# Grouped-query attention on one Trainium2 core: where the softmax's inverse sums are applied, and in which order TensorE does a unit's work

## What is computed

```python
def block_gqa_attention(q, k, v):
    ...
    def one_block(qb):
        s = jnp.einsum('bqkgd,bskd->bkgqs', qb, k).astype(jnp.float32) * scale
        p = jax.nn.softmax(s, axis=-1).astype(v.dtype)
        return jnp.einsum('bkgqs,bskd->bqkgd', p, v)
```

## Time and profile before

| what | value |
|---|---|
| median of 3 runs | 3661.1 us (3657.92 to 3663.45) |
| span of the profiled execution | 3665.8 us |
| this stage, first score product to last output | 1451.9 to 1843.2 us |
| TensorE, whole program | busy 3414.6 us, 93% of the span |
| VectorE, whole program | busy 1622.0 us, 44% |
| ScalarE, whole program | busy 815.3 us, 22% |
| GpSimd, whole program | busy 366.0 us, 10% |
| LDWEIGHTS (PEld), whole program | busy 1749.2 us, 48% |

### The profile page before, as it was taken

One profiled execution on the slowest core, in us unless ns is written; L12 is line 12 of the kernel. 1 busy time (PEld: TensorE's weight loads), 2 busy tenths in 40 slices (PEclk: granted clock), 3 DMA queues, 4 the chain that ended last, 5 costly groups with the idle time before them and its releaser, 6 DMA issues. The chain is left out here.

```text
span 3665.8 us, 51705 instructions
## 1 busy us (share of the span) xinstructions
PE 3414.6 (93%) x20940; PEld 1749.2 (48%) x20940; DVE 1622.0 (44%) x2578; ACT 815.3 (22%) x1819; POOL 366.0 (10%) x355
## 2 busy tenths in 40 slices
PE   9999999898999799999998999998899979898996
PEld 4444665533333344777755333333455658554332
DVE  4750886511111475777756110113342875563214
ACT  0000660100000122555510000000333551110112
POOL 0010300210000000000000200000000820003110
PEclk9999999899999999999998999999999989999998
DMA  9990211699999621000024999997322302229996
GB/s 370 359 346 1 93 70 69 274 389 427 426 424 425 239 89 62 22 1 1 1 92 184 380 426 427 426 424 308 130 82 79 139 17 87 95 98 347 420 417 264
DMA packets 146709, 818.45 MB, mean 223 GB/s; under 512 B 29763, under 2 KB 35651, under 8 KB 100390
## 3 DMA queue, kind: packets, MB, share of 16 engines
q1 hardware_dynamic: 117910, 737.25, 50.3%
q0 software_dynamic: 25824, 68.88, 4.9%
q10 hardware_dynamic: 2736, 8.95, 0.6%
HBM read 752.56 MB, written 82.56 MB: 228 GB/s over the span
## 5 line engine op out<-in xcount | busy, mean ns | idle before, releaser
L2415 PE MATMUL m_yp<-m_w,m_hidT 128*32 128x512 f32 (+2 forms) x2248 | 378.5, 595 | 10.3 <-issue 4.3
L2392 PE MATMUL m_up<-m_w,m_xT 128*32 128x512 f32 (+2 forms) x1792 | 313.9, 612 | 36.3 <-DMA m_w<-in_moe_w_up 33.9
L2392 PE MATMUL m_gp<-m_w,m_xT 128*32 128x512 f32 (+2 forms) x1792 | 297.4, 594 | 4.7 <-DVE m_xT L1978 2.9
L2143 DVE TENSOR_TENSOR m_hid<-m_sg,m_up 128x512 f32<-128x512 f32 x42 | 28.9, 688 | 561.4 <-PE m_up L2392 561.4
L2138 DVE TENSOR_TENSOR m_yt<-m_yp,keep_flat 128x512 f32<-128x512 f32 x128 | 82.5, 687 | 392.5 <-PE m_yp L2415 391.7
L2415 PEld LDWEIGHTS m_yp<-m_w,m_hidT 128*32 128x32 f32 (+2 forms) x2248 | 121.7, 124 | 219.0 <-issue 213.5
L2392 PEld LDWEIGHTS m_up<-m_w,m_xT 128*32 128x32 f32 (+2 forms) x1792 | 106.7, 127 | 238.4 <-issue 238.3
L2476 ACT ACTIVATE m_sg<-m_gp 128x512 f32<-128x512 f32 (+1 forms) x64 | 33.5, 524 | 759.7 <-PE m_gp L2392 515.2
L434 PE MATMUL front_acc<-front_hT,front_wt 128*128 128x512 f32 x448 | 194.7, 594 | 0.4 <-DVE q0T L535 0.4
L1233 PE MATMUL n_acc<-n_wt,n_hT 128*128 128x512 f32 (+2 forms) x512 | 191.2, 529 | 2.1 <-DMA n_wt<-in_w_in 1.4
L2392 PEld LDWEIGHTS m_gp<-m_w,m_xT 128*32 128x32 f32 (+2 forms) x1792 | 97.7, 123 | 198.2 <-issue 194.6
(11 more groups left out here) (520 smaller groups left out, 5037.4 us busy)
## 6 DMA issues: line engine op xcount, KB each, us to landing
m_w<-in_moe_w_gate SPq DMA_DIRECT2D x64, 2048.0 KB
m_w<-in_moe_w_up SPq DMA_DIRECT2D x64, 2048.0 KB
m_w<-in_moe_w_down SPq DMA_DIRECT2D x64, 2048.0 KB
v<-in_ada_w SPq DMA_DIRECT2D x40, 1024.0 KB
m_w<-in_moe_w_gate SPq DMA_DIRECT2D x32, 1024.0 KB
m_w<-in_moe_w_up SPq DMA_DIRECT2D x32, 1024.0 KB
m_w<-in_moe_w_down SPq DMA_DIRECT2D x32, 1024.0 KB
v<-in_w_mod SPq DMA_DIRECT2D x24, 1024.0 KB
```

What stands on the lines that cost most here:

```text
L2392: last = pe.matmul(acc[part, 0:F], xT[:, j, k, part], w[:, place_of[m_, r][0], k * F:(k + 1) * F], start=k == 0, stop=k == KC - 1)
L2415: last = pe.matmul(yp[e][part, :], hidT[:, k, part], w[:, place_of["d", r][0], k * D + e * 512:k * D + (e + 1) * 512], start=k == 0, stop= ...
```

## The change

The inverse sums are applied earlier and by another engine, and the order within a unit is another one:

- GpSimd, idle in this stage before, multiplies each head's row of 1024 exponentials in place by its inverse sum, two instructions a unit. TensorE's fills wait for that (`n_ready`) and no longer for the exponentials.
- VectorE's reciprocal is one column for each head, one instruction a head (before: one of 128 columns for a unit).
- The transpose of the inverse sums, ScalarE's copy of them (`spread`) and the buffer `inv_rows` are gone. VectorE's last step is a plain copy (`copy_out`) in place of the multiplication.
- TensorE's order is `score(n+1)`, all four fills of unit n, `combine(n-1)`. Fill 3 goes into the bank of fill 0, behind its copy. ScalarE copies fills 0 and 3, VectorE fills 1 and 2; ScalarE's copy of fill 0 of unit n now stands ahead of the exponentials of unit n+1.
- The maximum of the first head is taken in two halves and joined by a reduction of two columns: the first half starts when half of that head's scores are there (`s_half`).

```diff
                 def turn_probs(n):
+                    if n:
+                        copied(pe, n - 1, range(4))
+                    for f, bank in enumerate(BANKS):
+                        if f % 2 == 0:
+                            pe.wait_ge(n_ready, 2 * n + f // 2 + 1)
+                        if f == 3:
+                            copied(pe, n, (0,))
...
                 score(0)
                 for n in range(UNITS):
                     if n + 1 < UNITS:
                         score(n + 1)
-                    for i in range(3):
-                        turn_probs(n, i)
+                    turn_probs(n)
                     if n:
                         combine(n - 1)
-                    turn_probs(n, 3)
                 combine(UNITS - 1)
...
-                    pe.wait_ge(r_ready, n + 1)
-                    pe.transpose(out[:, P:2 * P], inv[:, n % 2].rearrange("p h w -> p (h w)"), ident[:, :]).then_inc(pv_done, 1)
...
+                    dve.wait_ge(s_half, n + 1)
+                    dve.tensor_reduce(parts[:, n % 2, 0:1], scores[0][:, 0:HALF], AX.X, ALU.max).then_inc(part_max, 1)
+                    dve.wait_ge(s_ready, 2 * n + 1)
+                    dve.tensor_reduce(parts[:, n % 2, 1:2], scores[0][:, HALF:], AX.X, ALU.max).then_inc(part_max, 1)
+                    dve.wait_ge(part_max, 2 * n + 2)
+                    dve.tensor_reduce(top[:, n % 2, 0:1], parts[:, n % 2], AX.X, ALU.max, negate=True).then_inc(max_ready, 1)
+                    dve.wait_ge(s_ready, 2 * n + 2)
+                    dve.tensor_reduce(top[:, n % 2, 1:2], scores[1][:, :], AX.X, ALU.max, negate=True).then_inc(max_ready, 1)
+
+                def inverse(n, h):
+                    dve.wait_ge(p_ready, 2 * n + h + 1)
+                    dve.reciprocal(inv[:, n % 2, h:h + 1], total[:, n % 2, h:h + 1]).then_inc(inv_ready, 1)
...
                     if n + 1 < UNITS:
                         row_max(n + 1)
-                    evacuate_probs(dve, n, 0, dve.tensor_copy)
-                    evacuate_probs(dve, n, 2, dve.tensor_copy)
+                    evacuate(dve, n, 1, dve.tensor_copy, evac_v)
+                    if n + 1 < UNITS:
+                        inverse(n + 1, 0)
+                    evacuate(dve, n, 2, dve.tensor_copy, evac_v)
+                    if n + 1 < UNITS:
+                        inverse(n + 1, 1)
                     if n:
-                        scaled_out(n - 1)
-                    if n + 1 < UNITS:
-                        inverse(n + 1)
-                scaled_out(UNITS - 1)
+                        copy_out(n - 1)
+                copy_out(UNITS - 1)
...
                 exponentials(0)
                 for n in range(UNITS):
+                    evacuate(act, n, 0, copy, evac_s)
                     if n + 1 < UNITS:
                         exponentials(n + 1)
-                    evacuate_probs(act, n, 1, copy)
-                    if n:
-                        spread(n - 1)
-                    evacuate_probs(act, n, 3, copy)
-                spread(UNITS - 1)
+                    evacuate(act, n, 3, copy, evac_s)
+
+            @block.gpsimd
+            def _(pool):
+                for n in range(UNITS):
+                    for h in range(2):
+                        pool.wait_ge(inv_ready, 2 * n + h + 1)
+                        pool.tensor_scalar(probs[:, n % 2, h], probs[:, n % 2, h], inv[:, n % 2, h:h + 1], None, ALU.mult).then_inc(n_ready, 1)
```

More of the change, by code:

```diff
@@ L128, in pair_attention, with copied @@
         probs = st.sb("probs", [P, 2, 2, S])
-        probsT = st.sb("probsT", [P, 2, 2, TILES, P])
+        probsT = st.sb("probsT", [P, 2, 2 * TILES * P])
+        parts = st.sb("parts", [P, 2, 2])
         top = st.sb("top", [P, 2, 2])
         total = st.sb("total", [P, 2, 2])
-        inv = st.sb("inv", [P, 2, 2, HEAD])
-        inv_rows = st.sb("inv_rows", [P, P])
+        inv = st.sb("inv", [P, 2, 2])
         scores = [st.ps(f"scores{h}", [P, S]) for h in range(2)]
-        turn = [st.ps(f"turn{b}", [P, 512]) for b in range(TURN)]
+        turn = [st.ps(f"turn{b}", [P, 512]) for b in range(3)]
         out = st.ps("out", [P, 512])
         ahead_in = st.sem("ahead_in")
[L138 to L148, removed]
+        s_half, s_ready, part_max, max_ready, p_ready = (st.sem(n) for n in ("s_half", "s_ready", "part_max", "max_ready", "p_ready"))
+        inv_ready, n_ready = st.sem("inv_ready"), st.sem("n_ready")
+        t_done, evac_v, evac_s = st.sem("t_done"), st.sem("evac_v"), st.sem("evac_s")
+        pv_done, o_done = st.sem("pv_done"), st.sem("o_done")
+        BANKS, BY_ACT, BY_DVE = (0, 1, 2, 0), (0, 3), (1, 2)
+        def copied(eng, n, fills):
+            for done, mine in ((evac_s, BY_ACT), (evac_v, BY_DVE)):
+                count = sum(f in fills for f in mine)
+                if count:
+                    eng.wait_ge(done, len(mine) * n + max(i for i, f in enumerate(mine) if f in fills) + 1)
         with st.block() as block:
@@ L159, in _ @@
             def _(pe):
[L160 to L165, removed]
                 def score(n):
@@ L173, in score, with turn_probs @@
                                 pe.wait_ge(p_ready, 2 * (n - 1) + h + 1)
-                            last = pe.matmul(scores[h][:, c * 512:(c + 1) * 512], qT[half, j, t * P:(t + 1) * P],
-                                             kT[half, 2 * j // SHARE, c * 512:(c + 1) * 512], start=True, stop=True)
+                            last = pe.matmul(scores[h][:, c * HALF:(c + 1) * HALF], qT[half, j, t * P:(t + 1) * P],
+                                             kT[half, 2 * j // SHARE, c * HALF:(c + 1) * HALF], start=True, stop=True)
                             if c == 1:
                                 last.then_inc(s_ready, 1)
[L179 to L183, removed]
+                            elif h == 0:
+                                last.then_inc(s_half, 1)
+                def turn_probs(n):
+                    if n:
[5 more added lines that the diff above has]
+                            copied(pe, n, (0,))
+                        for m in range(4):
+                            k = f % 2 * 4 + m
+                            last = pe.transpose(turn[bank][:, m * P:(m + 1) * P], probs[:, n % 2, f // 2, k * P:(k + 1) * P], ident[:, :])
+                        last.then_inc(t_done, 1)
                 def combine(n):
@@ L219, in row_max, with copy_out @@
                 def row_max(n):
[L220 to L229, removed]
+                    dve.wait_ge(s_half, n + 1)
[9 more added lines that the diff above has]
+                    dve.reciprocal(inv[:, n % 2, h:h + 1], total[:, n % 2, h:h + 1]).then_inc(inv_ready, 1)
+                def copy_out(n):
                     j, t = n // TILES, n % TILES
-                    dve.wait_ge(rb_done, n + 1)
-                    dve.tensor_tensor(natural[:, j, t], grid(out[:, 0:P]), grid(inv_rows[:, :]), ALU.mult).then_inc(o_done, 1)
+                    dve.wait_ge(pv_done, n + 1)
+                    dve.tensor_copy(natural[:, j, t], out[:, 0:P].rearrange("p (r c) -> p r c", c=GRID_W // TILES)).then_inc(o_done, 1)
                 row_max(0)
-                inverse(0)
+                for h in range(2):
+                    inverse(0, h)
                 for n in range(UNITS):
```

27 lines of the change are left out of this document (10 added, 17 removed).

## The result

The changed kernel takes 3722.97 us (median of four runs), beside 3662.27 us for the kernel before: the ratio is 1.0154, 95% interval 1.014 to 1.0168. One of the four runs was a slow one (4232.4 us, at a mean granted clock of 0.789 where the others have 0.962); it counts in the median and not in the ratio. By the medians the change costs 61 us, by the ratio 56 (51 to 62), where 12.5 us less was forecast; 3722.97 lies above the range, which ended at 3690.

A forecast was written before the change was run, and what follows sets the result against it. TensorE was taken to bound the kernel at 5.97 us a unit; 63 x 0.19 = 12.0 and 0.5 at the stage's end gave -12.5 us, so 3648.6 us, range 3644 to 3690.

The forecast's parts named there:

- What bounds the kernel, and TensorE's unit: TensorE bounds the stage at 5.97 us a unit; turning and split fills go, saving 0.19 (0.17 to 0.21), leaving 5.78.
- The clock of one unit: Times after a unit's scores start: first exponential 3.11, first reciprocal to 4.9, GpSimd 5.0, next scores 5.78 us.
- G: GpSimd's time for one multiplication of 128x1024, two a unit; taken as 1.3 us.
- 4.03 + G: Unit time in us once the third fill waits for GpSimd's second multiplication; as long as before, 5.97, at G = 1.94.
- The border of 1.73: Value of G in us under which GpSimd's second multiplication is hidden; beyond it the third fill waits.
- G, bounded: GpSimd's multiplication estimated from other rows: 1.16 from below, 2.5 from above, 1.3 us taken, nearer to MEMSET.
- The prediction's other estimate, 1.84 us: GpSimd's multiplication at about 1.8 cycles an element at 1.2 GHz, with 0.3 us fixed; unit 5.87, sum near -6 us.
- The sum: Whole kernel: 63 x 0.19 = 12.0 and 0.5 at the stage's end, -12.5 us, giving 3648.6.
- Rival (b): GpSimd becomes the bound, third fill waits for the second multiplication: slower, 3689 us at 2.36, 3698 at 2.5; chance 0.22.
- rival (a): GpSimd a little too slow, G between 1.73 and 2.05: 3652 us at 1.8, 3661 at 1.94, +7 at 2.05; chance 0.13.
- The end of the stage: Last scores to last output: 10.88 + 2G, 13.5 us at G = 1.3, against 13.98 before, 0.5 less.
- The start, and contention: Unit 0 has 3.8 us before its fills, so no gain or loss; SBUF contention kept within G's upper end.

The follow-up runs named there:

- the square: Four kernels' unit times: kernel before 5.97 us; new order with inverse sums still turned 6.00; two_input with TensorE's former order 5.86; two_input 5.75.
- two_input: Changed kernel with GpSimd's TENSOR_SCALAR replaced by a TENSOR_TENSOR with the inverse sum broadcast along the row; ratio 0.9968 to the kernel before.
- cols768: Changed kernel with GpSimd scaling only the first 768 of each head's 1024 columns, the rest left unscaled; ratio 1.0028 to the kernel before.

## Why the prediction was wrong, step by step

**What bounds the kernel, and TensorE's unit.** Right, and a little low: 0.19 a unit was taken, and the unit without waits is 5.74 to 5.75, 0.22 less than 5.97. The bounds of 0.17 and 0.21 came from adding a turning and a rounding of the fill; the square shows that the terms don't add.

**The clock of one unit.** Right. The first exponential starts 3.11 behind the scores (1655.24 - 1652.13), as worked out. The first reciprocal starts at 4.55 and GpSimd at 4.79, where 4.9 and 5.0 were said. Two units take 1665.56 - 1652.13 = 13.43, which less two multiplications of 2.84 leaves 7.74, so the loop is T = 3.87 + G instead of 4.03 + G. The border of 1.73 was therefore too low by 0.15 or more (5.75 - 3.87 = 1.88, and two_input has no wait at 1.89).

**G, bounded.** This is the step that failed. The forecast put G at 1.3 and it is 2.843. The row of TENSOR_SCALAR on 24 columns had the instruction itself (with a comparison and a product in one), 326 ns, and it was read as nearly all fixed cost because CAST took 200; the slope was then borrowed from MEMSET, with the reason that the reads are what doubles the price. The measured 2.50 ns a column with 0.28 fixed gives 0.34 for 24 columns: the small row was in line with the true slope and couldn't tell it from the borrowed one. Reads aren't what counts either: COPY reads one stream at 1036 ns, TENSOR_SCALAR one stream at 2842, TENSOR_TENSOR two at 2360. The upper end of 2.5 assumed that no elementwise form is dearer by the column than the two-input one, and this one is: 2.50 ns for 2.11. The trace of the kernel before had one more row that speaks to it, the two-input form on the same 24 columns:

```profile
L2254 POOL TENSOR_TENSOR keep_flat<-keep_flat 128x24 f32<-128x24 f32 x2 | 0.5, 237 | 0.2
```

At equal width TENSOR_SCALAR was the dearer of the two, 326 for 237 ns. By the later figures the 89 are the difference of the fixed costs (0.28 and 0.19), so this row gives no slope; but it was a warning that the two-input rows needn't bound the other form from above.

The Trainium skill, GPSIMD Engine Reference, § 4.1 Engine selection, calls one-input work on GpSimd roughly line rate. An estimate from it, at one column a cycle of the 1.2 GHz that the same page gives, is 853 ns for 1024 columns. COPY with its 1036 ns, fixed cost included, is near that; TENSOR_SCALAR isn't: its 2.50 ns a column are 3.0 cycles of the same clock. The prediction's other estimate, 1.84 us, is short of 2.84 as well. Here the measurement decides.

**The sum.** With the measured G the prediction's own formulas give T = 6.87, 63 x 0.90 = 56.7, an end of 10.88 + 5.69 = 16.6 (+2.6), together +59; the stage has +55. That these are so close is in part luck: the formula's unit is 0.16 too long (63 x 0.16 = 10), and it knows nothing of the three long pairs (4.9) and of the slower end (1.1). Rival (b), slower through the third fill's wait for the second multiplication, is what happened, in its place and form and beyond the price that it named; it had 0.22. The mechanism was right and the error lies in the one duration. The range ended at TENSOR_TENSOR's 2.36 us, though the prediction wrote 2.5 and 3698 for it. (Two slips decide nothing: 2.11 x 1024 is 2.16 and not 2.18, and rival (a) leaves out the end of the stage, 0.5 at G = 1.8 and 1.0 at 2.05.)

**The end of the stage.** 17.66 for the formula's 16.6. The clock explains the difference: behind the wait of 1.96 us on GpSimd and around the one of 1.66 the granted clock is 0.65 from 1893 to 1896 and 0.78 from 1896 to 1899. The last eight transposes take 1.97 where the eight ahead of them took 1.07; from them to the product with v it is 1.90 (1894.20 to 1896.10) for the formula's 0.97, and from that product to the last one 2.94 (to 1899.04) for 2.36. That is 1.5 more, of which GpSimd's earlier start and end give back 0.4.

**The start, and contention.** The start was right: GpSimd's first two multiplications take 5.69 us there and the fills of unit 0 don't wait for them; these fills start 9.0 behind the first scores (1464.16 - 1455.15), where it was 10.4. VectorE's rows didn't grow beside GpSimd's (692 for a half maximum, as in the earlier trace rows). The Trainium skill, SBUF — State Buffer, § Who interferes with whom, says that a VectorE instruction with at most one SBUF input outside its two-port modes doesn't contend with GpSimd; the trace agrees, since VectorE's inputs here are PSUM or, one at a time, a column or two in SBUF, and GpSimd's 128 instructions lie within 2835 to 2857 ns.

## What to carry to other kernels

Before work goes to an engine that has none, measure that very instruction at that size: a row of the same operation on 24 columns, or another operation on the right size, isn't a bound. An engine that stands in a loop of several others binds long before it is full, here from about a third of the unit for each of its two instructions (between 1.89 and 2.20 of 5.75 us); work out the loop, and price the step for which it starts to cost. And if a duration decides the sign, try the other forms of the same computation: here one of them was a third shorter.

## What the runs showed of the hardware

- On GpSimd, at 128x1024 in float32: MEMSET 0.95 us, COPY 1.04, TENSOR_TENSOR with one column broadcast 1.89, with two full tiles 2.36, TENSOR_SCALAR 2.77 with a constant and 2.84 with a scalar for each partition.
- A short stretch of transposes between two kinds of products costs TensorE 0.10 to 0.14 us beside its length: the square of 5.97, 6.00, 5.86 and 5.75.
- Behind waits of TensorE the granted clock fell. In the changed kernel it is 0.66 over 1620 to 1625, a mean of TensorE's two levels of 1.2 and 2.4 GHz, and three pairs of units took 15.05 in place of 13.43; each of the three lies in a stretch of 50 us with a granted clock of 0.97. In the kernel before and in cols768, where TensorE is busy 288.24 of 300 us, the same 300 us show 1.00. A wait alone doesn't bring it about: from 1500 to 1800 us TensorE waits 23 times for GpSimd, 1.66 us or so each time, and the clock fell behind two of them. No run took TensorE's waits away and kept the clock apart, so that the waits are the cause is read from the order in time alone.
